# Tile 0 of a PEER layer: every fourth value row weighed by TensorE, with two PSUM banks fewer for the other matmuls

## The chip, the cores and the metric

The kernel runs on one core of one Trainium2 chip. The metric is the device time of one execution in microseconds (us). TensorE is called PE below (PEld is its weight load), VectorE is DVE, ScalarE is ACT, GpSimd is POOL and SyncE is SP, as in the profile.

## The reference

One transformer layer over 512 tokens of width 1024, all float32:

```python
xn   = rmsnorm(h, norm1_g); proj = xn @ w_in
h    = h + concat(forgetting_attention(8 heads), differential_attention(4 heads, 2 maps each)) @ w_out
hn   = rmsnorm(h, norm2_g)
q    = hn @ w_q                              # 8 heads, two halves of 128
eidx = two-stage top-16 of q . sub_keys      # 16 experts per token and head, of 16384
hid  = gelu(sum_d u_tab[eidx] * hn) * softmax(top scores)
h    = h + sum_k hid[k] * v_tab[eidx[k]]     # the value rows
out  = rmsnorm(h, final_g)
```

The last part (PEER) gathers, for each token, 8 x 16 rows of u and of v. With 128 tokens (one per partition) as a tile, "one row" below is a gathered 128 x 1024 block: its own expert row for each of the 128 tokens.

## The kernel before

There are four token tiles. Tile 0 makes attention, projections and queries by itself; tiles 1 to 3 make them together as a second group. PEER of tile 0 runs beside the second group's attention, output projection and queries ("hosted"), since its gathers keep DMA busy; PEER of tiles 1 to 3 follows with nothing beside it ("the tail").

The hosted stretch is 32 slots of four rows each (8 heads x 4 groups). A slot has nine gaps. In DVE's order, slot k holds the dots of its own four u rows in gaps 0, 2, 4, 6 (`dot`, L1220), the coefficients of the slot before at gap 1 (`coefs`, L1234) and the adds of the slot before's four v rows in gaps 1, 3, 5, 7 (`add_row`, L1244: h += coef * row). ACT makes the gelu (L928) of the slot's four dots at gap 6. The second group's work is cut into pieces, and a planner with fixed cost shares lays the pieces into the gaps; PE, ACT and DVE each run their part of every piece in this one order, in program order on each engine. By this plan slots 0 to 5 hold tile 0's last queries and the first input projections of tiles 1 to 3; slots 6 to 16 projections and the forgetting attention; slots 17 to 23 the differential attention and most of the output projection; slots 24 to 31 the last output piece, the second norm and the queries. Slots 25 to 31 hold about two `query` pieces (L609, 16 matmul records each) and one `keys` piece (L694, three tiles of four records each) per slot. DVE has no part in `query` and `keys`: ACT copies them out (L877, L888). Of these, query 8 of head 4 stands at gap 2 of slot 28, the keys piece of head 3 at gap 5 and query 9 at gap 7.

PSUM has eight banks: `mm` is a ring of three (mm0, mm1, acc0) that all 160 projection-like results go through in order, `sc_b` a ring of three (sc0, sc1, acc1) for the 64 score maps, `tr` and `o` one each. PE may fill result n only when result n-3 has been copied out. In the profile the third bank of either ring shows as `acc`. A query's or projection's weights are slabs of 1 MB that SP loads (L490) into two places of `w_ring`; a slab is loaded once PE has done with the slab two before it.

POOL issues the hosted gathers in one order: for each row i, u of row i+4 (L531; waits until dot i is done), then v of row i (L538; waits until the add of row i-4 is done). u and v have rings of four rows each. POOL then issues the tail's gathers (L552), which bring u and v of a row together (1 MB) into a ring of 12 places; places 0 to 3 need nothing but their indices, places 4 to 7 (u_ring, v_ring) wait until all hosted dots and adds are done.

In the tail DVE makes the dots (L1228), ACT turns the four coefficients of a group into diagonal matrices (`diag`, L935), and PE adds `diag @ row` into acc0 and acc1, both halves, over all 128 rows of a tile (L760, four matmul records per row). So that the first tile end can use the same code as the others, DVE clears acc0 and acc1 (L1345) after the hosted stretch, and `fin_tile` (L1263) adds acc to h.

## Time and profile before

| | |
|---|---|
| median of 3 runs | 1662.96 us (1656.92 to 1666.79) |
| the profiled execution | 1672.45 us, span 1670.7 us |
| mean granted TensorE clock | 0.895 |
| busy over the span | PE 77%, PEld 40%, DVE 70%, ACT 26%, POOL 47% |
| HBM | 355 GB/s over the span |

The profiled execution is 9.5 us (0.6%) above the median, and 1.8 us of it lies outside of the span. Busy shares are averages over stages of different kind, so the stages have to be read one by one.

### The profile page before, as it was taken

The page shows a single profiled execution, that of the slowest core. Times are in us where ns is not written, and L with a number is a line of the kernel's source. Part 1 is how long each engine was busy: PE and PEld are TensorE (multiplying, and loading weights), DVE is VectorE, ACT ScalarE, POOL GpSimd, SP SyncE. Part 2 cuts the span into 40 slices and gives each one's busy share as a digit, 9 for nine tenths or more (in the row PEclk, how much of TensorE's full clock was granted, in tenths as well). Part 3 has the DMA queues.
Part 4 walks back from the last instruction along what each step waited for, and adds up shares of the span by engine and source line. Part 5 has one row for each costly group of instructions (what it writes and reads, how often), then busy time and mean ns, then how long its engine had stood idle before and what let it go on. Part 6 is the DMA issues. An engine that isn't in the chain of part 4 may idle for free.

```text
span 1670.7 us, 12756 instructions
## 1 busy us (share of the span) xinstructions
PE 1290.0 (77%) x3547; PEld 662.5 (40%) x3547; DVE 1168.5 (70%) x2794; ACT 427.8 (26%) x1045; POOL 787.5 (47%) x650
## 2 busy tenths in 40 slices
PE   6885788899567788577877877876787777777786
PEld 5754556557333455233323333332333333233332
DVE  2125758898899977676666667666676686666664
ACT  2322313333342321222222222222222222222221
POOL 0004545667455675454554444455444454455441
PEclk9987898798677899799999988999999989999999
DMA  9628888899677898899999999999999999999994
GB/s 309 195 78 295 299 310 302 278 330 345 233 262 250 297 390 322 324 422 421 422 421 421 421 422 422 421 422 422 421 422 421 421 397 421 422 422 421 420 423 168
DMA packets 141244, 594.38 MB, mean 356 GB/s; under 512 B 12400, under 2 KB 53368, under 8 KB 92024
## 3 DMA queue, kind: packets, MB, share of 16 engines
q0 software_dynamic: 92160, 536.91, 80.3%
q1 hardware_dynamic: 49016, 56.67, 10.3%
q8 instruction: 30, 0.49, 0.1%
q14 instruction: 38, 0.31, 0.0%
HBM read 591.44 MB, written 2.10 MB: 355 GB/s over the span
## 4 chain that ended last, share of the span: by engine, by line
DMA 28%; DVE 17%; PE 17%; ACT 2%; issue 2%; POOL 0%; DVEq 0%; POOLq 0%
PE acc L760 11%; DMA act_mem<-in_peer_uv_dram,eidx 11%; DMA v_ring<-in_peer_uv_dram,eidx 9%; DMA map_mem<-in_peer_uv_dram,eidx 8%; PE mm L609 3%; PE acc L609 2%; DVE act_mem L1228 2%; DVE v_ring L1228 2%; DVE map_mem L1228 2%; DVE v_all L1228 1%; DVE w_ring L1228 1%; DVE u_ring L1228 1%; DVE onehot L1195 1%; DVE onehot L1188 1%; DVE picked L1199 1%
## 5 line engine op out<-in xcount | busy, mean ns | idle before, releaser
L531 POOL DMA_INDIRECT u_ring<-in_peer_u_dram,eidx x128 | 162.0, 1266 | 259.0 <-DVE gneg L1205 130.1
L928 ACT ACTIVATE gel<-hid 128x4 f32<-128x4 f32 x128 | 26.2, 205 | 766.9 <-DVE hid L1228 723.1
L760 PE MATMUL acc<-v_all,diag 128*128 128x512 f32 x256 | 142.1, 707 | 84.8 <-ACT diag L935 84.8
L538 POOL DMA_INDIRECT v_ring<-in_peer_v_dram,eidx x128 | 154.6, 1207 | 93.0 <-DVE h L1244 64.1
L760 PE MATMUL acc<-u_ring,diag 128*128 128x512 f32 x256 | 138.4, 692 | 75.1 <-ACT diag L935 75.1
L760 PE MATMUL acc<-w_ring,diag 128*128 128x512 f32 x256 | 137.3, 687 | 74.5 <-ACT diag L935 74.5
L1244 DVE SCALAR_TENSOR_TENSOR h<-v_ring,coef,h 128x1024 f32<-128x1024 f32 x128 | 164.3, 1283 | 4.0 <-DMA v_ring<-in_peer_v_dram,eidx 0.6
L1220 DVE CUSTOM_DVE_ANT_0 u_ring<-u_ring,hn 128x1024 f32<-128x1024 f32 x128 | 156.0, 1218 | 8.8 <-DMA u_ring<-in_peer_u_dram,eidx 8.5
L552 POOL DMA_INDIRECT u_ring<-in_peer_uv_dram,eidx x64 | 77.7, 1215 | 146.9 <-PE acc L760 129.0
L552 POOL DMA_INDIRECT w_ring<-in_peer_uv_dram,eidx x64 | 80.9, 1264 | 131.5 <-PE acc L760 127.8
L552 POOL DMA_INDIRECT v_all<-in_peer_uv_dram,eidx x64 | 78.2, 1222 | 128.9 <-PE acc L760 125.8
L609 PE MATMUL mm<-act_mem,w_ring 128*128 128x384 f32 x336 | 122.0, 521 | 13.2 <-DMA w_ring<-in_w_in_dram 4.8
L935 ACT ACTIVATE diag<-ident,coef 128x128 f32<-128x128 f32 x384 | 123.5, 390 | 29.8 <-DVE coef L1234 22.0
L760 PEld LDWEIGHTS acc<-v_all,diag 128*128 128x128 f32 x256 | 55.2, 226 | 170.0 <-issue 155.1
L760 PEld LDWEIGHTS acc<-u_ring,diag 128*128 128x128 f32 x256 | 53.9, 221 | 159.3 <-issue 154.8
L1228 DVE CUSTOM_DVE_ANT_0 v_ring<-v_ring,hn 128x1024 f32<-128x1024 f32 x64 | 77.8, 1224 | 55.1 <-DMA v_ring<-in_peer_uv_dram,eidx 54.9
L760 PEld LDWEIGHTS acc<-w_ring,diag 128*128 128x128 f32 x256 | 53.4, 219 | 157.7 <-issue 153.3
L760 PE MATMUL acc<-v_ring,diag 128*128 128x512 f32 x256 | 115.1, 592 | 0.0
L760 PE MATMUL acc<-map_mem,diag 128*128 128x512 f32 x256 | 115.1, 592 | 0.0
L760 PE MATMUL acc<-act_mem,diag 128*128 128x512 f32 x256 | 115.1, 592 | 0.0
L1228 DVE CUSTOM_DVE_ANT_0 map_mem<-map_mem,hn 128x1024 f32<-128x1024 f32 x64 | 77.7, 1223 | 53.0 <-DMA map_mem<-in_peer_uv_dram,eidx 52.9
L1228 DVE CUSTOM_DVE_ANT_0 act_mem<-act_mem,hn 128x1024 f32<-128x1024 f32 x64 | 77.7, 1224 | 51.3 <-DMA act_mem<-in_peer_uv_dram,eidx 51.3
(212 smaller groups left out, 2243.6 us busy)
## 6 DMA issues: line engine op xcount, KB each, us to landing
w_ring<-in_w_in_dram SPq DMA_DIRECT2D x18, 1024.0 KB
w_ring<-in_peer_w_q_dram SPq DMA_DIRECT2D x16, 1024.0 KB
v_ring<-in_w_in_dram SPq DMA_DIRECT2D x6, 1024.0 KB, 12.2
w_ring<-in_w_out_dram SPq DMA_DIRECT2D x6, 1024.0 KB
h<-in_x_dram SPq DMA_DIRECT2D x4, 512.0 KB, 6.5
v_ring<-in_w_out_dram SPq DMA_DIRECT2D x2, 1024.0 KB, 5.0
u_ring<-in_peer_u_dram,eidx POOLq DMA_INDIRECT x128
v_ring<-in_peer_v_dram,eidx POOLq DMA_INDIRECT x128
```

The lines of the kernel that those rows point to most:

```text
L531: nc.gpsimd.indirect_dma_start(out=u_ring[:, c % U_RING, :], out_offset=None, in_=peer_u[0], in_offset=bass.IndirectOffsetOnAxis(ap=eidx[n ...
L538: nc.gpsimd.indirect_dma_start(out=v_ring[:, c % V_RING, :], out_offset=None, in_=peer_v[0], in_offset=bass.IndirectOffsetOnAxis(ap=eidx[n ...
L552: nc.gpsimd.indirect_dma_start(out=row_mem[place], out_offset=None, in_=peer_uv, in_offset=bass.IndirectOffsetOnAxis(ap=eidx[n % 3][:, c:c ...
L609: last = nc.tensor.matmul(bk[:, 0:n], w[:, c, q * P:(q + 1) * P], actT[:, c, 0:n], start=(c == 0), stop=(c == KC - 1))
L760: last = nc.tensor.matmul(acc[half][:, :], diag[:, c % COLS, :], v_row(n, c)[:, half * BANK:(half + 1) * BANK], start=(n % PH == 0 and c = ...
L928: nc.scalar.activation(gel[:, par, g0:g0 + COLS], hid[:, par, g0:g0 + COLS], ACT.Gelu).then_inc(gelu_done, 1)
L935: nc.scalar.activation(diag[:, c, :], ident[:, :], ACT.Copy, scale=coef[:, par, g0 + c:g0 + c + 1]).then_inc(diag_done, 1)
L1188: nc.vector.tensor_tensor(out=onehot[:, :, :], in0=top_hlf[:, :, :].rearrange("p a b -> p (a b)").unsqueeze(2).broadcast_to([P, 2 * TOPK, ...
L1195: nc.vector.tensor_tensor(out=oh, in0=oh, in1=tk_if[:, q, :].unsqueeze(1).broadcast_to([P, TOPK, TOPK]), op=ALU.mult).then_inc(topk_step, 1)
L1220: nc.vector.tensor_tensor_reduce(out=u_ring[:, c % U_RING, :], in0=u_ring[:, c % U_RING, :], in1=hn[:, :], scale=1.0, scalar=0.0, op0=ALU. ...
L1228: nc.vector.tensor_tensor_reduce(out=u_row(n, c), in0=u_row(n, c), in1=hn[:, :], scale=1.0, scalar=0.0, op0=ALU.mult, op1=ALU.add, accum_o ...
L1244: nc.vector.scalar_tensor_tensor(out=ht, in0=v_ring[:, c % V_RING, :], scalar=coef[:, par, c:c + 1], in1=ht, op0=ALU.mult, op1=ALU.add).th ...
```

## The change

In tile 0 every fourth value row (c = 3, 7, 11, 15 of each head, 32 of 128) is no longer added by DVE. ACT makes its diagonal (`mixed_diag`, in gap 4 of the next slot, the last one after all pieces), and PE adds it into acc0 and acc1 (`mixed_row`, in gap 7 of the next slot, the last one after all pieces), with a semaphore of its own, `v_mixed`. acc0 and acc1 are in use from the first of these rows on, so the rings `mm` and `sc_b` shrink to two banks each for the whole kernel. The gather of such a row waits for `v_mixed` of the one before, the other gathers count DVE's adds without them (`used`). The clearing of acc0 and acc1, with the waits before it, goes. Tile 0's end waits for both semaphores. Slabs, pieces, gaps and shares stay. The diff, without a few counting lines:

```diff
@@ -381,8 +381,8 @@
         acc = [bank("acc0"), bank("acc1")]
-        mm = [bank("mm0"), bank("mm1"), acc[0]]
-        sc_b = [bank("sc0"), bank("sc1"), acc[1]]
+        mm = [bank("mm0"), bank("mm1")]
+        sc_b = [bank("sc0"), bank("sc1")]
         tr_b = bank("tr")
         o_b = bank("o")
@@ -451,6 +452,15 @@
             return w
         HOSTED = HOSTS * PH * TOPK
+
+        MIXED = HOSTED // COLS
+
+        def used(n, c):
+
+            i = TOPK * n + c
+            if i < HOSTED:
+                return (COLS - 1) * (i // COLS) + min(i % COLS + 1, COLS - 1)
+            return i + 1 - MIXED
         def row_place(n, c):
@@ -534,7 +544,10 @@
             def gather_v(n, c):
                 if n or c >= V_RING:
-                    pool.wait_ge(v_used, TOPK * n + c + 1 - V_RING)
+                    if c % COLS == COLS - 1:
+                        pool.wait_ge(v_mixed, GRP * n + c // COLS)
+                    else:
+                        pool.wait_ge(v_used, used(n, c - V_RING))
                 nc.gpsimd.indirect_dma_start(
                     out=v_ring[:, c % V_RING, :], out_offset=None, in_=peer_v[0],
                     in_offset=bass.IndirectOffsetOnAxis(ap=eidx[n % 3][:, c:c + 1], axis=0)).then_inc(v_in[c % V_RING], 16)
@@ -543,10 +556,11 @@
                 place, lap = row_place(n, c)
                 if lap > 1:
-                    pool.wait_ge(v_used, TOPK * n + c + 1 - ROW_RING)
+                    pool.wait_ge(v_used, used(n, c - ROW_RING))
                 elif place == EARLY_ROWS:
                     pool.wait_ge(dot_done, HOSTED)
-                    pool.wait_ge(v_used, HOSTED)
+                    pool.wait_ge(v_used, used(PH * HOSTS - 1, TOPK - 1))
+                    pool.wait_ge(v_mixed, MIXED)
                 elif place == FREED_ROWS:
                     pool.wait_ge(mm_full, len(MM))
                 nc.gpsimd.indirect_dma_start(
@@ -755,11 +769,22 @@
                         pe.wait_ge(acc_drained, 2 * (n // PH))
                     place, lap = row_place(n, c)
                     pe.wait_ge(row_in[place], 16 * lap)
-                    pe.wait_ge(diag_done, TOPK * n + c + 1 - HOSTED)
+                    pe.wait_ge(diag_done, MIXED + TOPK * n + c + 1 - HOSTED)
                     for half in range(2):
                         last = nc.tensor.matmul(acc[half][:, :], diag[:, c % COLS, :], v_row(n, c)[:, half * BANK:(half + 1) * BANK],
                                                 start=(n % PH == 0 and c == 0), stop=(n % PH == PH - 1 and c == TOPK - 1))
                     last.then_inc(v_used, 1)
+
+            def mixed_row(k):
+
+                c = COLS * (k % GRP) + COLS - 1
+                pe.wait_ge(v_in[c % V_RING], 16 * (k + 1))
+                pe.wait_ge(diag_done, k + 1)
+                for half in range(2):
+                    last = nc.tensor.matmul(acc[half][:, :], diag[:, k % COLS, :],
+                                            v_ring[:, c % V_RING, half * BANK:(half + 1) * BANK],
+                                            start=(k == 0), stop=(k == MIXED - 1))
+                last.then_inc(v_mixed, 1)
             pe.wait_ge(pool_const, 6)
             pe.wait_ge(g1_in, 16)
@@ -770,8 +795,11 @@
                 for n in range(PH * tile, PH * tile + PH):
                     for grp in range(GRP):
                         for gap in range(GAPS):
+                            if gap == 2 * COLS - 1 and (n or grp):
+                                mixed_row(GRP * n + grp - 1)
                             for p_ in pieces_in(n, grp, gap):
                                 piece(*p_)
+            mixed_row(MIXED - 1)
             for n in range(PH * HOSTS, HEADS):
                 for grp in range(GRP):
                     peer_group(n, grp * COLS)
@@ -931,9 +959,20 @@
                 gelu(n, par, g0)
                 act.wait_ge(coef_done, GRP * n + g0 // COLS + 1)
                 for c in range(COLS):
-                    act.wait_ge(v_used, TOPK * n + g0 + c + 1 - COLS)
+                    if TOPK * n + g0 < HOSTED + COLS:
+                        act.wait_ge(v_mixed, MIXED)
+                    else:
+                        act.wait_ge(v_used, used(n, g0 + c - COLS))
                     nc.scalar.activation(diag[:, c, :], ident[:, :], ACT.Copy,
                                          scale=coef[:, par, g0 + c:g0 + c + 1]).then_inc(diag_done, 1)
+
+            def mixed_diag(k):
+                act.wait_ge(coef_done, k + 1)
+                if k >= COLS:
+                    act.wait_ge(v_mixed, k + 1 - COLS)
+                c = COLS * (k % GRP) + COLS - 1
+                nc.scalar.activation(diag[:, k % COLS, :], ident[:, :], ACT.Copy,
+                                     scale=coef[:, k // GRP % 2, c:c + 1]).then_inc(diag_done, 1)
             def fin_rt(t):
                 act.wait_ge(fin_step, FIN * t + 1)
@@ -948,6 +987,8 @@
                 for n in range(PH * tile, PH * tile + PH):
                     for grp in range(GRP):
                         for gap in range(GAPS):
+                            if gap == 2 * COLS - 4 and (n or grp):
+                                mixed_diag(GRP * n + grp - 1)
                             if gap == 2 * COLS - 2:
                                 gelu(n, n % 2, grp * COLS)
                             for p_ in pieces_in(n, grp, gap):
@@ -956,6 +997,7 @@
                             fin_rt(tile - 1)
                         if grp == 2:
                             gate_exp(n + 1)
+            mixed_diag(MIXED - 1)
             for n in range(PH * HOSTS, HEADS):
                 for grp in range(GRP):
                     peer_group(n, n % 2, grp * COLS)
@@ -1330,19 +1375,15 @@
                             elif gap < GAPS - 1 and k > 0:
                                 if c == 0:
                                     coefs(*behind)
-                                add_row(behind[0], behind[1], behind[2] + c)
+                                if c < COLS - 1:
+                                    add_row(behind[0], behind[1], behind[2] + c)
                             if k == PH * GRP * tile and gap == GAPS - 1 and tile:
                                 fin_tile(tile - 1)
                             for p_ in pieces_in(n, grp, gap):
                                 piece(*p_)
                 coefs(n, par, grp * COLS)
-                for c in range(COLS):
+                for c in range(COLS - 1):
                     add_row(n, par, grp * COLS + c)
-
-                dve.wait_ge(*emptied(MM[-1]))
-                dve.wait_ge(*emptied(next(u for u in reversed(MM) if u[0] not in ON_SCALAR)))
-                for half in range(2):
-                    link(nc.vector.memset(acc[half][:, :], 0.0))
             for n in range(PH * HOSTS, HEADS):
                 t, par = n // PH, n % 2
                 if n % PH == 0:
```

## Rows read from the trace of the kernel before

**Rows 1.** Busy sums by stretch: start:end length, PE PEld DVE ACT POOL, clock, DMA share, GB/s.

```profile
0.00:137.30 137.30, 106.91 (x451) 80.22 (x452) 38.47 (x131) 37.97 (x110) 5.50 (x14) 0.91 0.62 197
137.30:255.60 118.30, 93.11 (x328) 62.20 (x327) 77.51 (x164) 29.97 (x61) 56.86 (x49) 0.86 0.83 297
255.60:420.90 165.30, 148.66 (x598) 100.56 (x596) 146.16 (x300) 59.84 (x126) 107.53 (x89) 0.88 0.91 323
420.90:555.00 134.10, 89.56 (x269) 46.24 (x270) 123.73 (x271) 47.58 (x97) 69.96 (x55) 0.75 0.73 251
555.00:686.30 131.30, 104.90 (x372) 64.86 (x370) 99.73 (x188) 30.84 (x69) 82.53 (x65) 0.92 0.92 336
686.30:1670.70 984.40, 746.87 (x1536) 308.43 (x1536) 682.88 (x1745) 221.60 (x583) 465.11 (x380) 0.92 0.98 407
```

**Rows 2.** Chain that ended last: start us, us, what.

```profile
721.96 13.78 DMA v_ring<-in_peer_uv_dram,eidx
...
1635.11 18.40 DMA act_mem<-in_peer_uv_dram,eidx
...
1655.78 7.12 PE acc L760 x16
```

**Rows 3.** Timeline at the hosted stretch's end: start us, us, engine line op tiles [idle before <-releaser].

```profile
681.67 0.16 DVE L1234 TENSOR_TENSOR coef<-gel,gate 128x4 f32<-128x4 f32 x1 [7.49 <-ACT gel L928]
...
681.92 5.53 DVE L1244 SCALAR_TENSOR_TENSOR h<-v_ring,coef,h 128x1024 f32<-128x1024 f32 x4
...
687.56 0.48 DVE L1345 MEMSET acc<- 128x512 f32 x1
688.23 0.94 POOL L552 DMA_INDIRECT u_ring<-in_peer_uv_dram,eidx  x1 [11.79 <-DVE h L1244]
```

**Rows 4.** DVE's timeline in slot 12: adds between dots.

```profile
349.98 1.28 DVE L1244 SCALAR_TENSOR_TENSOR h<-v_ring,coef,h 128x1024 f32<-128x1024 f32 x1
351.19 1.22 DVE L1220 CUSTOM_DVE_ANT_0 u_ring<-u_ring,hn 128x1024 f32<-128x1024 f32 x1
```

**Rows 5.** ACT's diagonals, line L935: min/median/max ns.

```profile
L935 ACT ACTIVATE diag<-ident,coef x384: 384/386/402, 695.2 to 1656.1; 128x128 f32<-128x128 f32 x192
```

**Rows 6.** PE's timeline in the query stage.

```profile
607.25 5.40 PE L609 MATMUL mm<-act_mem,w_ring 128*128 128x384 f32 x16 [1.83 <-issue]
...
622.50 7.09 PE L609 MATMUL acc<-act_mem,w_ring 128*128 128x384 f32 x16 [1.99 <-issue]
...
649.14 5.40 PE L609 MATMUL mm<-act_mem,w_ring 128*128 128x384 f32 x16 [1.39 <-ACT qyT L877]
...
664.38 7.09 PE L609 MATMUL acc<-act_mem,w_ring 128*128 128x384 f32 x16 [3.34 <-issue]
```

**Rows 7.** Timeline of DVE and PE in slots 28 and 31.

```profile
622.09 1.27 DVE L1244 SCALAR_TENSOR_TENSOR h<-v_ring,coef,h 128x1024 f32<-128x1024 f32 x1
...
630.32 0.61 PE L694 MATMUL acc<-subkT,qyT 128*128 128x128 f32 x4
...
668.98 1.28 DVE L1244 SCALAR_TENSOR_TENSOR h<-v_ring,coef,h 128x1024 f32<-128x1024 f32 x1
...
674.12 5.40 PE L609 MATMUL mm<-act_mem,w_ring 128*128 128x384 f32 x16 [1.32 <-ACT store L888]
```

**Rows 8.** PE's waits for score banks, 137 to 690 us: us in total, times, longest.

```profile
PE sc L719 <- DVE negmax L1102: 15.7, 4, 7.8
```

**Rows 9.** Timeline of SP, PE and ACT around the keys of head 4.

```profile
636.12 12.03 SPq L490 DMA_DIRECT2D w_ring<-in_peer_w_q_dram  x2
...
641.09 0.61 PE L694 MATMUL acc<-subkT,qyT 128*128 128x128 f32 x4
641.29 0.49 ACT L877 ACTIVATE qyT<-mm 128x384 f32<-128x384 f32 x1 [4.67 <-PE mm L609]
...
641.53 1.06 PE L694 MATMUL mm<-subkT,qyT 128*128 128x128 f32 x8
641.73 0.38 ACT L888 ACTIVATE store<-acc 128x256 f32<-128x256 f32 x1
```

10 lines of the change are left out of this document (7 added, 3 removed).

## The prediction

> **What bounds the kernel now.** I read the busy sums by stretch first, because the whole-span shares mix stages. The span falls into the part before the hosted rows (0 to 137.3 us), four hosted stretches (slots 0 to 5, 6 to 16, 17 to 23, 24 to 31 with the stretch's end), and the tail from 686.3 us on [rows 1]. In the tail DMA is busy 98% at 407 GB/s, and the chain that ended last alternates between a gather and the group that waited for it, from 721.96 to the last 7.12 us of matmuls [rows 1, 2]. The change touches nothing there. The tail starts with the gather of place 4, issued at 688.23 when the hosted adds had ended [rows 3], so its end moves one for one with the end of the hosted adds, and the question is only where that lies.
>
> In the hosted stretches no single engine is the bound; the reader is to see how the order of the two busiest changes [rows 1]:
> - slots 0 to 5, 118.3 us: PE 93.1, DVE 77.5, DMA 83%: PE first.
> - slots 6 to 16, 165.3 us: PE 148.7, DVE 146.2, DMA 91%: all three at about nine tenths.
> - slots 17 to 23, 134.1 us: DVE 123.7 (92%), PE 89.6 (67%): DVE alone.
> - slots 24 to 31, 131.3 us: PE 104.9, DVE 99.7, DMA 92%: PE's query pieces, and its waits for a slab between them [rows 6].
>
> **What one moved row costs and saves.** DVE: an add takes 1.28 us, but the next dot starts 1.21 us after it [rows 4], so 1.2 us is saved per row, 38 us over 32. PE: four rows are the 16 matmul records of 7.12 us in the chain [rows 2], so 1.78 us per row back to back. A query piece took 5.40 us after one wait and 7.09 after another [rows 6], the difference that the lower of the clock's two levels (1.2 and 2.4 GHz) makes in part of a piece; 32 rows are 57 us, more where the mean clock is below 1. ACT: one diagonal is 0.39 us [rows 5], 12 us in all, with ACT busy a quarter to a third [rows 1]: hidden as time, not as order (below). So 1.2 us on one engine is traded for 1.8 on another, and the place decides: it pays where DVE alone bounds, and costs where PE does. By the plan 5, 11, 7 and 8 of these rows fall into the four stretches, and the last one behind all pieces.
>
> **Stretch by stretch, against the profiled execution's 1672.45 us.**
>
> Before 137.3 us no row moves, but both bank rings are shorter. The nearest rows are those of the keys, where a fill began 0.25 us before the result two before it was copied out [rows 9]; by the order of the pieces some ten fills and the eight score maps of tile 0's differential attention follow that closely here, 18 x 0.25 = 4.5 us. PE is busy 106.9 of 137.3 us [rows 1], and the rest is waits for slabs and for the norms, which hides part. I take +1.5; bounds 0 and +5.
>
> Slots 0 to 5: 5 x 1.78 = +9 on PE, less what fits into its waits (25 us of idle, partly for slabs), and 5 x 1.2 = -6 where DVE leads. PE leads, with waits that hold about half of its part. +3; bounds -6 and +9.
>
> Slots 6 to 16: PE would need 148.7 + 11 x 1.78 = 168.3 us in 165.3, DVE 146.2 - 13.2 = 133. Part of PE's time is the low clock (0.88 on average), and with fewer waits some of this comes back: at the full clock the same work is 148.7 x 0.88 = 131 us. DVE was as full as PE, so its share pays too. +4; bounds -13 (all of the adds) and +20 (all of the rows).
>
> Slots 17 to 23: 7 x 1.2 = -8.4 for DVE. PE has 44 us of idle for 7 x 1.78 = 12 us and, at a clock of 0.75 [rows 1], up to 17. The score ring loses a bank just where every step fills two maps; PE already waits 15.7 us for DVE to empty sc0 and sc1, up to 7.8 at a time [rows 8], in which time DVE is busy with other work, so most of a longer wait costs nothing, but the maps come later after it. -6; bounds -8.4 and +5.
>
> Slots 24 to 31: 8 x 1.78 = +14.2 on PE, which is the path here. The keys piece of three tiles ran through three banks; with two, the second tile waits until ACT has copied the query (641.29 + 0.49 = 641.78 against its start at 641.53), the third until the first is copied [rows 9], and ACT has a diagonal to make between: some 0.5 us for each of 8 heads, +4. Against this stand PE's waits for slabs, 1.83, 1.99, 1.39 and 3.34 us [rows 6]: a slab is asked for when PE ends the one two before it (at 648 us) and used at 664.38 [rows 6, 9], so some 2.2 us more work per slab (1.78 and the copies' half) fills each of the waits by up to 2.2 us, -7.4 in all, and one of the two slow restarts (7.09 - 5.40) goes, -1.7. Slot 24 is DVE work, -1.2. That is +8. Then the release: PE runs behind DVE here. In slot 28 the fourth add started at 622.09, but PE ends the keys piece, behind which the moved row stands, at 630.9 [rows 7]. In slot 31 the add ended at 670.3 and PE gets to the place, behind query 15, at 679.5 [rows 7]: the lag grows from 7.5 to 9.2 us. POOL issues in one order, so behind the gather that waits for this row the next u and v gathers queue too, on a DMA that is 92% busy. I take +2 for it. +10; bounds +1 and +24.
>
> The end: three adds instead of four in 5.53 us, -1.4 [rows 3]. The clearing (from 687.56) stands behind the adds, beside the gathers, and frees nothing that the tail waits for. The last moved row ends on PE at about 684 to 686.5 us, no later than DVE's third add. -1.3; bounds -2.5 and 0.
>
> The wait for the row's diagonal is new on PE, and everything that PE has queued stands behind it. DVE makes the coefficients at gap 1 and ACT the diagonal at gap 4, PE comes to it at gap 7; only where PE is more than six gaps ahead of DVE, in a stretch led by DVE, does it wait, and there DVE is late anyway. I cost it at nothing; without that cover it would be up to 2 us in such a slot.
>
> Sum: 1.5 + 3 + 4 - 6 + 10 - 1.3 = +11.2 us. That is 1683.7 for the profiled execution and, put on the median, 1662.96 + 11 = 1674 us.
>
> **Two rules of the Trainium skill.** In the slots 6 to 16 PE is busy 90% by its matmuls, and its weight loads 100.6 of 165.3 us, 61% [rows 1]. The Trainium skill, Perfetto Trace Analysis, section "Identifying the Most-Contended Engine", holds that the busy share of matmuls is no measure of how near PE is to its limit, and wants the weight loads' share beside it. By that rule PE has room for the rows there, and the stretch would end at its bound of -13 instead of +4; this is rival 1.
> The clock in the slots 17 to 23 is 0.75 against 0.88 before [rows 1], where PE waits for emptied banks. The Trainium skill, TensorE: Matmul & The Clock Gate, section "A second HAM failure mode: psum-queue depth-cycling", says that going round a few PSUM banks leaves TensorE idle briefly and so often that its clock falls again and again, which costs throughput. This speaks against the change; it is the slow rival below.
>
> **The rivals.**
> 1. DVE's time pays wherever it is at nine tenths, and PE's rows vanish in its waits and in a better clock. For it: PE's idle time in the four hosted stretches is 549 - 436.2 = 113 us [rows 1] against 57 to be placed, and 148.7 us of PE time hold only 131 us of full-clock work. Against it: in the query stage the idle time is not there. It gives 1.5 - 3 - 13 - 8 + 8 - 1.3 = -16: 1647 us.
> 2. Slower by much: two banks take PE's lead. If in the slots 6 to 16 the clock fell from 0.88 to the 0.75 of the next stretch, PE's 131 us would take 175 instead of 149, +26 before a row is added, of which I count half, with +12 for the rows; with the late releases (+14 in the query stage) and nothing gained in the slots 17 to 23: 2 + 5 + 25 + 0 + 14 - 1 = +45, 1708 us; with a quarter of the clock's effect 1701. It decides from where PE's wait for an emptied bank lasts longer than PE was ahead of the engine that empties it; the longest such wait now is 7.8 us [rows 8].
> 3. Nothing measurable: DMA is the real limit of the slots 6 to 16 and 24 to 31 (91 and 92%), and both engines' shifts fall into its slack: +1 + 1 + 0 - 5 + 5 - 1 = +1, 1664 us.
>
> **How the numbers follow.** The forecast has 0.42 (its own range 1665 to 1684), rival 1 has 0.20, rival 2 has 0.17, rival 3 has 0.21. The likeliest gives 1674 us. The range is 1645 to 1701: it takes in rivals 1 and 3 and rival 2 up to its milder form, and leaves out some 0.17. About 0.5%, 8.3 us, is what a measurement of this kernel can tell from no change. Faster by more: rival 1 and a little of the rest, 0.22. Within it: rival 3 and the forecast's lower third, 0.32. Slower by more: 0.46.
>
> **What would show it.** In the profile after, DVE has 96 adds at L1244 and PE 128 more matmul records; the same six stretches should read: slots 17 to 23 shorter, slots 24 to 31 longer, slots 6 to 16 within a few us, with PE busy above 95% there. POOL's waits at the v gather should name PE where they named DVE. The forecast is wrong if the slots 6 to 16 shrink by ten us or more (then PE's busy time was no measure), if PE's clock falls below 0.85 there (then the banks count), or if the query stage does not grow (then the slab waits had room for all).

## The result and the profile after

The changed kernel takes 1692.12 us (median of 4 runs, 1690.5 to 1693.0) against 1664.8 for the one before: a ratio of 1.0158, 95% interval 1.0124 to 1.0191, some 26 us slower. The prediction was 1674 with a range of 1645 to 1701 and slower as the likeliest sign. So the sign held and the size fell short by more than half: the result lies outside the forecast's own range (1665 to 1684) and inside the stated one only by the room that was left for the milder form of rival 2. The profiled execution took 1691.76 us with a span of 1690.0 us, 19.3 above the span before; the profiled execution of before was itself above its median, so the tables of spans show some 7 us less than the medians do. Every experiment below was timed beside fresh executions of the kernel before, whose median was 1665.6 to 1670.5 us by the occasion; so the kernels are compared by their ratios to it, and a difference of two raw medians can be off by some 4 us.

The busy sums of the changed kernel in the same six stretches, cut where a slot's first dot starts on DVE and where the tail's normalized input starts (start:end length, PE PEld DVE ACT POOL, clock, DMA share, GB/s):

```profile
0.00:136.00 136.00, 106.80 (x450) 79.24 (x451) 38.57 (x131) 38.18 (x110) 5.44 (x14) 0.92 0.62 199
136.00:257.00 121.00, 100.06 (x336) 64.81 (x335) 71.55 (x159) 31.52 (x65) 53.53 (x49) 0.87 0.82 289
257.00:428.90 171.90, 164.41 (x653) 105.10 (x651) 132.76 (x288) 63.44 (x137) 104.22 (x89) 0.96 0.89 318
428.90:565.30 136.40, 94.67 (x290) 50.03 (x291) 115.94 (x265) 49.09 (x103) 65.68 (x55) 0.79 0.70 238
565.30:700.70 135.40, 119.82 (x414) 72.30 (x413) 90.76 (x180) 34.64 (x79) 75.40 (x65) 0.95 0.85 298
700.70:1690.00 989.30, 754.02 (x1540) 310.83 (x1538) 681.62 (x1743) 222.03 (x583) 457.33 (x382) 0.91 0.99 409
```

The last cut lies at the start of the tail's input here. For before, the same cut is at 688.7 us, 2.4 later than in [rows 1]:

```profile
555.00:688.70 133.70, 104.90 (x372) 64.86 (x370) 101.85 (x190) 30.84 (x69) 83.01 (x66) 0.91 0.90 330
688.70:1670.70 982.00, 746.87 (x1536) 308.43 (x1536) 680.76 (x1743) 221.60 (x583) 464.63 (x380) 0.92 0.98 408
```

Against [rows 1] and these two, the stretches changed by -1.3, +2.7, +6.6, +2.3, +1.7 and +7.3 us. DVE lost its adds everywhere (146.2 to 132.8 in slots 6 to 16), and no hosted stretch became shorter for it. PE took the rows (148.7 to 164.4, 96% of the stretch).

What became of the saved time stands in DVE's waits. In slots 6 to 16 of before, then of the changed kernel (us in total, times, longest):

```profile
DVE map_mem L1102 <- PE sc L723: 8.5, 3, 4.1
DVE map_mem L1102 <- PE acc L723: 5.8, 4, 2.6
```

```profile
DVE map_mem L1144 <- PE sc L737: 30.1, 10, 7.9
DVE rinv L1161 <- PE o L762: 5.4, 1, 5.4
```

DVE was busy 13.4 us less there and waited 21 us more for score maps and for attention's output. Slot 7 shows two such waits, where before it had one of 4.09 us; first PE's, then DVE's timeline of the changed kernel (start us, us, engine, line, tiles, [idle before <-releaser]):

```profile
266.37 1.88 PE L784 MATMUL acc<-v_ring,diag 128*128 128x512 f32 x4
268.09 3.62 PE L615 MATMUL mm<-w_ring,act_mem 128*128 128x256 f32 x16
...
280.89 7.01 PE L623 MATMUL mm<-act_mem,w_ring 128*128 128x384 f32 x16
287.73 1.88 PE L784 MATMUL acc<-v_ring,diag 128*128 128x512 f32 x4
289.54 0.70 PE L733 MATMUL sc<-store 64*128 64x256 f32 x2
```

```profile
273.34 0.42 DVE L1144 CUSTOM_DVE_ANT_0 map_mem<-sc,act_mem 128x256 f32<-128x256 f32 x1 [4.03 <-PE sc L737]
...
290.81 0.42 DVE L1144 CUSTOM_DVE_ANT_0 map_mem<-sc,act_mem 128x256 f32<-128x256 f32 x1 [7.94 <-PE sc L737]
```

The moved row at 287.73 stands between a projection piece and the scores that DVE's next step needs. Before, the scores followed the projection at once. A row takes under 2 us, so it makes only about half of the second wait's growth (4.09 to 7.94); the rest is that PE was already behind when it came to the projection, at 280.89 instead of 276.53 us, and the row of slot 6 (266.37), with which the slot starts, is a part of that. The slot grew from 16.9 to 23.1 us. It is the one that grew most: slots 8 and 9 behind it were 4.5 us shorter together, and over slots 6 to 16 6.6 us are left. In slots 17 to 23 it is the output projection that comes late (before, where a result can also lie in the third bank, `acc`, then after):

```profile
DVE h L1077 <- PE mm L669: 3.7, 3, 3.1
DVE h L1077 <- PE acc L669: 1.2, 1, 1.2
```

```profile
DVE h L1119 <- PE mm L683: 14.4, 6, 3.7
```

[Rows 8] shows PE's waits for two of the three score banks. The third stands in a row of its own; here it is, and behind it the changed kernel's, which has two banks only:

```profile
PE acc L719 <- DVE negmax L1102: 7.5, 1, 7.5
```

```profile
PE sc L733 <- DVE negmax L1144: 27.2, 9, 8.4
```

So with a bank less PE waits 27.2 us instead of 23.2 for DVE to empty a score bank, and no wait is much longer than before.

At the end of the hosted stretch, answering [rows 3], POOL and DVE of the changed kernel:

```profile
695.86 0.94 POOL L551 DMA_INDIRECT v_ring<-in_peer_v_dram,eidx  x1 [8.45 <-PE acc L784]
697.10 1.63 POOL L566 DMA_INDIRECT v_all<-in_peer_uv_dram,eidx  x1 [0.30 <-issue]
...
704.06 0.94 POOL L566 DMA_INDIRECT u_ring<-in_peer_uv_dram,eidx  x1 [1.25 <-PE acc L784]
...
736.62 1.85 POOL L566 DMA_INDIRECT u_ring<-in_peer_uv_dram,eidx  x1 [10.02 <-PE acc L774]
```

```profile
696.64 4.12 DVE L1287 SCALAR_TENSOR_TENSOR h<-v_ring,coef,h 128x1024 f32<-128x1024 f32 x3
700.68 1.28 DVE L1294 SCALAR_TENSOR_TENSOR hn<-h,rstd,g2b 128x1024 f32<-128x1024 f32 x1
704.60 1.23 DVE L1271 CUSTOM_DVE_ANT_0 v_all<-v_all,hn 128x1024 f32<-128x1024 f32 x1 [2.64 <-DMA v_all<-in_peer_uv_dram,eidx]
```

The gather of the last moved row (695.86) waited 8.45 us for PE's row before it, and the tail's first four gathers stand behind it in POOL's one order. Before, the tail's first gather went out at 671.8, 17 us ahead of the tail's input; here it is 3.6 us ahead, and the first dots wait for their rows. The last moved row itself waited 2.79 us for its gather and ended on PE at 703.3, 2.5 us behind DVE's third add; the gather of place 4 (704.06) waits for it. The tail's 17th gather (the one at 736.62) stood at 717.31 before. From it to the end both kernels take 953.4 us. So all 19.3 us lie ahead of it: 12.0 up to the tail's input, and 7.3 between that and the 17th gather (28.6 us before, 35.9 after).

One limit of these tables: kernels with the same order of work up to a place can be compared up to there. Three of those below have one order up to slot 17, and single executions of them take 164.7, 164.8 and 167.7 us in slots 6 to 16. The changed kernel and the one where the tail's gathers go first have one order up to the last value gather, and take 171.9 and 178.3 there. So a difference of one pair under 3 us says nothing by itself, and one of 6 to 7 can be chance too. That slots 6 to 16 grow with the rows on PE rests on many kernels: the eight that have full or thin rows there, or their work, read 171.6 to 186.5, and the six that don't read 161.7 to 167.7.

### The profile page after: what moved, and what is told of

Its sections match the earlier page's. It is cut to its first block, busy times and chain, and to the rows that moved or that the text cites. A ratio compares the mean times of both kernels' runs of the same rounds, so it can differ in the third digit from the quotient of the medians.

```text
span 1690.0 us, 13041 instructions
## 1 busy us (share of the span) xinstructions
PE 1339.8 (79%) x3675; PEld 682.3 (40%) x3675; DVE 1131.2 (67%) x2760; ACT 438.9 (26%) x1077; POOL 761.6 (45%) x650
## 4 chain that ended last, share of the span: by engine, by line
DMA 28%; PE 21%; DVE 15%; ACT 2%; issue 2%; POOL 1%; DVEq 0%; POOLq 0%
PE acc L774 12%; DMA map_mem<-in_peer_uv_dram,eidx 12%; DMA act_mem<-in_peer_uv_dram,eidx 9%; DMA v_ring<-in_peer_uv_dram,eidx 7%; PE mm L623 5%; PE mm L683 2%; DVE act_mem L1271 2%; DVE map_mem L1271 1%; DVE v_ring L1271 1%; PE acc L784 1%; DVE u_ring L1271 1%; DVE w_ring L1271 1%; DVE onehot L1237 1%; DVE onehot L1230 1%; DVE picked L1241 1%
## 5 line engine op out<-in xcount | busy, mean ns | idle before, releaser
L541 POOL DMA_INDIRECT u_ring<-in_peer_u_dram,eidx x128 | 150.0, 1172 | 256.0 <-DVE gneg L1248 128.9
L551 POOL DMA_INDIRECT v_ring<-in_peer_v_dram,eidx x128 | 149.2, 1166 | 138.7 <-PE acc L784 64.9
L774 PE MATMUL acc<-w_ring,diag 128*128 128x512 f32 x256 | 145.0, 719 | 76.5 <-ACT diag L966 71.8
L623 PE MATMUL mm<-act_mem,w_ring 128*128 128x384 f32 x512 | 174.8, 499 | 3.2 <-DVE act_mem L1055 1.6
L566 POOL DMA_INDIRECT w_ring<-in_peer_uv_dram,eidx x64 | 73.7, 1152 | 140.6 <-PE acc L774 138.5
L966 ACT ACTIVATE diag<-ident,coef 128x128 f32<-128x128 f32 x384 | 123.9, 390 | 31.5 <-DVE coef L1277 22.0
L623 PEld LDWEIGHTS mm<-act_mem,w_ring 128*128 128x128 f32 x512 | 98.8, 196 | 74.7 <-issue 12.4
L1287 DVE SCALAR_TENSOR_TENSOR h<-v_ring,coef,h 128x1024 f32<-128x1024 f32 x96 | 123.1, 1283 | 4.5 <-DMA v_ring<-in_peer_v_dram,eidx 0.6
L615 PE MATMUL mm<-w_ring,act_mem 128*128 128x256 f32 x416 | 107.2, 418 | 7.2 <-DVE act_mem L1055 5.1
```

Source lines behind the costliest of these rows:

```text
L541: nc.gpsimd.indirect_dma_start(out=u_ring[:, c % U_RING, :], out_offset=None, in_=peer_u[0], in_offset=bass.IndirectOffsetOnAxis(ap=eidx[n ...
L551: nc.gpsimd.indirect_dma_start(out=v_ring[:, c % V_RING, :], out_offset=None, in_=peer_v[0], in_offset=bass.IndirectOffsetOnAxis(ap=eidx[n ...
L566: nc.gpsimd.indirect_dma_start(out=row_mem[place], out_offset=None, in_=peer_uv, in_offset=bass.IndirectOffsetOnAxis(ap=eidx[n % 3][:, c:c ...
L615: last = nc.tensor.matmul(bk[:, 0:SLAB], actT[:, c, j * P:(j + 1) * P], w[:, c, :], start=(c == 0), stop=(c == KC - 1))
L623: last = nc.tensor.matmul(bk[:, 0:n], w[:, c, q * P:(q + 1) * P], actT[:, c, 0:n], start=(c == 0), stop=(c == KC - 1))
L774: last = nc.tensor.matmul(acc[half][:, :], diag[:, c % COLS, :], v_row(n, c)[:, half * BANK:(half + 1) * BANK], start=(n % PH == 0 and c = ...
```

## The experiments

The theory at the start (Theory A in the first expectations) was that the rows on TensorE carry most of the loss and the rings a few us. Beside it stood the late release of the moved rows' buffer and the start of the tail.

### The rings alone, and the rows alone

```diff
-        mm = [bank("mm0"), bank("mm1"), acc[0]]
-        sc_b = [bank("sc0"), bank("sc1"), acc[1]]
+        mm = [bank("mm0"), bank("mm1")]
+        sc_b = [bank("sc0"), bank("sc1")]
```

> The kernel before with two banks in each ring and no row moved: one half of the change alone. Theory A (most of the 27 us comes from the moved rows: their PE time and the later releases) expects what the prediction gave the banks: 1.5 us before slot 0 and 4 us in the query stage, so +3 to +9 us over before. Theory B (the lost banks take PE's lead) expects at least half of the loss, +13 to +25 us, most of it in slots 6 to 23. If the banks cost nothing, within 2 us of before.

Measured: 1677.16 us, ratio 1.0058 (1.0032 to 1.0085), so some 10 us of the 26 (5 to 14).

The counterpart keeps the three-bank rings of the kernel before and has the rows:

```diff
-        mm = [bank("mm0"), bank("mm1")]
-        sc_b = [bank("sc0"), bank("sc1")]
+        mm = [bank("mm0"), bank("mm1"), acc[0]]
+        sc_b = [bank("sc0"), bank("sc1"), acc[1]]
...
+                pe.wait_ge(*emptied(MM[filled[0] - len(mm)]))
                 for half in range(2):
-                    last = nc.tensor.matmul(acc[half][:, :], diag[:, k % COLS, :],
+                    last = nc.tensor.matmul(mm[filled[0] % len(mm)][:, :], diag[:, k % COLS, :],
```

> The other half alone: the 32 rows go to PE in the same places, with the same waits and the same DVE saving, but both rings keep three banks. The moved rows are written into the mm bank that the next result will overwrite, so their part of tile 0's sum is left out, and acc0 and acc1 are cleared as before. Theory A expects +18 to +24 us over before (the change's 27 less the banks' 3 to 9). Theory B expects at most +13 us, or even a gain.

Measured: 1690.28 us, ratio 1.0149 (1.0095 to 1.0203). The rows bring nearly the whole loss with the longer rings too. With the rings' 10 us this makes 35 where 26 were measured; the intervals leave it open whether the two causes add. One part of this stays open: a row here has to find the next products' bank empty, a wait that the changed kernel doesn't have.

### The rows' time on PE

```diff
+                n = BANK if k == 0 else 8
                 for half in range(2):
-                    last = nc.tensor.matmul(acc[half][:, :], diag[:, k % COLS, :],
-                                            v_ring[:, c % V_RING, half * BANK:(half + 1) * BANK],
+                    last = nc.tensor.matmul(acc[half][:, 0:n], diag[:, k % COLS, :],
+                                            v_ring[:, c % V_RING, half * BANK:half * BANK + n],
```

> The change with PE's time for the moved rows taken away: 31 of the 32 rows are multiplied over 8 columns per half instead of 512 (the first over all), every wait, place, bank and the DVE saving stay. The rest of those rows is left out of tile 0's sum. If PE's 57 us of extra work is what costs, -15 to -27 us against the change. If the order costs (releases behind PE, the tail's first gathers behind the last moved row, DVE waiting for score maps), -3 to -10 us.

Measured: 1687.85 us, ratio 1.0128 (1.0082 to 1.0173), only 5 us under the changed kernel by the ratios (4 by the medians), less than their intervals can tell. The groups of PE in slots 6 to 16, first of the changed kernel, then of this one (xcount | busy us, mean ns of one | idle before):

```profile
L623 PE MATMUL mm<-act_mem,w_ring 128*128 128x384 f32 x128 | 46.1, 516 | 0.0
...
L784 PE MATMUL acc<-v_ring,diag 128*128 128x512 f32 x44 | 21.2, 604 | 2.1 <-DMA v_ring<-in_peer_v_dram,eidx 1.2 <-ACT diag L974 1.0
```

```profile
L623 PE MATMUL mm<-act_mem,w_ring 128*128 128x384 f32 x128 | 52.9, 576 | 0.0
...
L785 PE MATMUL acc<-v_ring,diag 128*128 128x8 f32 x44 | 6.1, 248 | 2.2 <-DMA v_ring<-in_peer_v_dram,eidx 1.2 <-ACT diag L975 1.0
```

The rows lost 15.1 us of PE time, and PE was busy 163.3 us instead of 164.4: the other pieces took 14 us more, with a granted clock of 0.88 instead of 0.96. So in these slots the run could not separate PE's time from its order; what the rows gave up in columns the clock took from the others. In slots 24 to 31 it was otherwise: PE was busy 112.1 us instead of 119.8, at a clock of 0.91 instead of 0.95, and the stretch took 129.4 us instead of 135.4.

### PE's work alone, and DVE's saving alone

These three take the change apart in another way. The first is the rings alone plus PE's work at the rows' places, which nothing waits for but the clearing of acc0 and acc1 at the end:

```diff
+            def more_pe(k):
+                for half in range(2):
+                    last = nc.tensor.matmul(acc[half][:, :], ident[:, :], g2b[:, half * BANK:(half + 1) * BANK],
+                                     start=(k == 0), stop=(k == GRP * PH * HOSTS - 1))
...
+                            if gap == 2 * COLS - 1 and (n or grp):
+                                more_pe(GRP * n + grp - 1)
```

> The kernel before with two-bank rings (as in the run of the rings alone), where TensorE also does 32 pairs of full-width products of the size and at the places of the moved rows, on resident data into the two free banks; nothing waits for them and nothing reads them, and VectorE still adds all four rows of a group. So TensorE's work is that of the change, without its releases and without what VectorE saves. The rings alone gave 1677 us. Theory P: TensorE's 57 us of added work lengthen slots 6 to 16 by 5 to 8 us and the rest by 2 to 6: 1685 to 1691. Theory R: TensorE's work alone costs little: 1677 to 1681, slots 6 to 16 at 164 to 167 us.

Measured: 1695.33 us, ratio 1.0155 (1.0117 to 1.0192). That is the whole loss of the change, with no late release and nothing saved. Against the rings alone, PE's added work costs 16 us by the ratios, give or take 8. Its slots 6 to 16:

```profile
263.00:435.80 172.80, 166.38 (x648) 105.90 (x646) 146.00 (x300) 60.07 (x126) 106.17 (x89) 0.94 0.89 315
```

DVE does all its adds here (146.0) and the stretch is as long as in the changed kernel, where it does three quarters of them (132.8 in 171.9). Theory P held: by the ratio the time is 1691 us on the scale of 1664.8, the upper end of what it gave. That PE alone sets the stretch is not shown by this, since the changed kernel also has late releases that may have taken what DVE's saving gave; the next run bears on it.

The second is the changed kernel with VectorE's saving undone, by adding each group's third row twice:

```diff
+                if c % COLS == COLS - 2:
+                    link(nc.vector.scalar_tensor_tensor(out=ht, in0=v_ring[:, c % V_RING, :], scalar=coef[:, par, c:c + 1], in1=ht,
+                                                        op0=ALU.mult, op1=ALU.add))
```

> The changed kernel, where VectorE adds the third row of each group twice, so that its work is again that of four adds (the third row counts double in tile 0's output; TensorE still weighs the fourth). It asks what VectorE's saving of 32 adds at 1.2 us, 38 us in sum, is worth. If it had been worth its length on the path, the time would rise by 38 us to 1730. The forecast put it on the path only in slots 17 to 23, worth about 6 us net and 9 us by itself. If the saved time only turns into waits for TensorE's results and for loads, the time stays within 4 us of 1692. I expect 3 to 8 us: 1695 to 1700, most of it in slots 17 to 23.

Measured: 1703.99 us, ratio 1.0229 (1.0184 to 1.0275). The saving is worth about 12 us in the changed kernel (3 to 21 by the two intervals), more than the 3 to 8 that I had expected, and not 38. In the profile it shows in slots 6 to 16 (178.9 us against 171.9) and 17 to 23 (139.1 against 136.4). The 7 us are no more than two executions of one order differed by above, but they are spread otherwise: eight of the eleven slots are each 1.0 to 1.6 us longer, about an add, where the chance difference lay in two slots. So DVE's adds still lie on the path in most slots there, and PE's time isn't the only bound.

The third is the change without its costs: the kernel before, with the fourth add cut to eight columns.

```diff
-                ht = h[:, n // PH, :]
-                nc.vector.scalar_tensor_tensor(out=ht, in0=v_ring[:, c % V_RING, :], scalar=coef[:, par, c:c + 1], in1=ht,
+                w = 8 if c % COLS == COLS - 1 else D
+                ht = h[:, n // PH, 0:w]
+                nc.vector.scalar_tensor_tensor(out=ht, in0=v_ring[:, c % V_RING, 0:w], scalar=coef[:, par, c:c + 1], in1=ht,
```

> The kernel before, with three-bank rings and no row on TensorE, where VectorE's add of a group's fourth row takes 8 of its 1024 columns in tile 0 (so that row is left out of the sum but for 8 columns); its gather, its buffer and the order are as before. It is the change without its costs, so it gives the most that moving the adds could be worth. The run with TensorE's added work alone and the changed kernel differ by 9.9 us in the length of the part with tile 0's work (710.6 against 700.7), and the changed kernel with VectorE's saving undone differs by the same 10 us (710.8). If the saving is worth the same here: 1655 (1651 to 1659), 2 to 4 us of it in slots 17 to 23. The forecast's terms put 9 us into slots 17 to 23 alone. If instead TensorE's rows hide a larger worth, and VectorE bounds more slots once nothing is added on TensorE, up to half of the 38 us comes out: 1640 to 1650.

Measured: 1659.69 us, ratio 0.9964 (0.9936 to 0.9992): the offload, free of charge, is worth 6 us, between 1 and 11. (An add of 8 columns isn't nothing: DVE was busy 33 us less in the hosted slots, against 38 less in the changed kernel.) Its slots 6 to 16 and 17 to 23:

```profile
248.60:410.30 161.70, 148.43 (x603) 100.68 (x601) 134.95 (x300) 59.89 (x126) 104.61 (x89) 0.89 0.93 330
410.30:541.30 131.00, 88.61 (x269) 46.04 (x270) 116.54 (x271) 46.97 (x97) 67.48 (x55) 0.75 0.75 257
```

Even in slots 17 to 23, where DVE was busy 92% [rows 1], 7.2 us less of DVE made the stretch 3.1 us shorter, which is at the edge of what a pair of executions can tell. DVE's waits for the output projection rose there from 4.9 to 9.1 us (both kinds of bank), with nothing added on PE. The largest difference was in slots 0 to 5, 113.2 us against 118.3.

### The late release

On PE and on ACT:

```diff
-                            if gap == 2 * COLS - 1 and (n or grp):
+                            if gap == 2 * COLS - 4 and (n or grp):
-                            if gap == 2 * COLS - 4 and (n or grp):
+                            if gap == 2 * COLS - 6 and (n or grp):
```

> The changed kernel with the diagonal of the moved row built at gap 2 and the row weighed at gap 4 of the slot behind, instead of gaps 4 and 7; the arithmetic is the same. So far: the two-bank rings alone cost about 10 us, the rows with three-bank rings 22 to 25 us, and rows of eight columns, which take hardly any of TensorE's time, gave back only 4 us. Theory R (release): what costs beside the banks is that the gather of a group's fourth row, and everything behind it on GpSimd's queue, waits for TensorE's row of the group before, which stands late in the slot. Then the release three gaps earlier cuts GpSimd's waits for TensorE (65 us in sum in the changed kernel) to about half, and the time falls by 5 to 9 us, to 1683 to 1687. Theory P (TensorE's time and order): what costs is that TensorE's own chain of pieces is longer in the slots where it works without a break. Then the earlier place changes nothing (within 3 us of 1692), or costs 2 to 5 us where the row now stands in front of scores that VectorE waits for.

Measured: 1712.74 us, ratio 1.0254 (1.0213 to 1.0294): 16 us slower than the change by the ratios (20 by the medians), where a gain of 5 to 9 or a loss of 2 to 5 was expected. GpSimd's waits for TensorE did fall, from 56 to 9 us. But now PE waits for the row itself, and everything behind it in PE's order waits too (waits between 136 and 690 us):

```profile
PE acc L784 <- DMA v_ring<-in_peer_v_dram,eidx: 23.4, 5, 7.4
```

```profile
DVE map_mem L1144 <- PE sc L737: 39.3, 13, 6.7
```

Slots 6 to 16 took 186.5 us. Of the two places, gap 7 is the better by far.

The next takes the release away instead, with a second buffer (`fin`) for every other moved row:

```diff
+        def mixed_mem(k):
+            return fin if k % 2 else v_ring[:, COLS - 1, :]
...
+                    if k > 1:
+                        pool.wait_ge(v_mixed, k - 1)
```

> The changed kernel, but the moved rows alternate between two buffers (the fourth place of the value ring, and the buffer of the final output, which nothing uses in tile 0), so that the gather of a moved row waits for the row two groups before, which is long done. Nothing else is changed. Theory R: GpSimd's waits for TensorE at the value gathers fall from 65 us to under 10 us, and what the late release cost comes back: 1692 falls to 1678 to 1684, with slots 6 to 16 at 165 to 168 us (171.9 in the changed kernel) and the stretch after tile 0's part 3 to 6 us shorter. Theory P: GpSimd's waits fall too, but slots 6 to 16 stay at 170 to 172 us, and only the start of the tail gains, 0 to 4 us: 1688 to 1692.

Measured: 1693.62 us, ratio 1.0152 (1.0113 to 1.0191), no gain. GpSimd's waits at that gather went:

```profile
POOL fin L554 <- PE acc L793: 0.6, 2, 0.3
```

and from the tail's input to its 17th gather it is 28.7 us again, 7.2 less than in the changed kernel. But slots 6 to 16 took 172.8 us, as theory P says, and slots 0 to 5 took 124.7 against 121.0, with 8.0 us of waits for weight slabs on PE against 1.0. These waits differ much from kernel to kernel in that stretch, 4.8 us in the one before and 7.1 in the one with the thin add. Whether the gathers, now free to go out sooner, delayed those slabs, or the execution fell so by chance, no run tells.

Two runs ask only for the end. In the first, the tail's first four gathers go ahead of the last value gather:

```diff
+                    if TOPK * n + c == HOSTED - 1:
+                        numbers_of(n + 1)
+                        for early in range(EARLY_ROWS):
+                            gather_row(n + 1, early)
```

> The change with one order altered: POOL issues the first four gathers of the tail before the last value gather of tile 0, which waits for the 31st moved row. In the profile after they stand behind it (697 to 702 us; before the change at 672 to 675 us, ahead of the end of the hosted stretch), DMA is idle meanwhile and the tail reads 989.3 us against 982.0. Theory A expects that these four rows (10 us of DMA) come back in large part: -5 to -9 us. If the tail's length differs for another reason (PE's clock, another restart of the rings), 0 to -2 us.

Measured: 1697.11 us, ratio 1.0181 (1.0138 to 1.0223): no gain that could be seen. The tail's gathers came earlier (the first at 694.2 with its input at 707.2), but the last moved row, now behind 4 MB of them, held PE:

```profile
710.74 3.78 PE L789 MATMUL acc<-v_ring,diag 128*128 128x512 f32 x4 [7.01 <-DMA v_ring<-in_peer_v_dram,eidx]
```

It ended at 714.5, and place 4's gather, which waits for it, went out at 715.3. The wait moved from one gather to the other. From the tail's input to its 17th gather it is 31.4 us, 4.5 less than in the changed kernel, but the rest took 960.7, the longest of all. Of the 9.3 us that this profiled execution lies above the changed kernel's, 6.4 are in slots 6 to 16, where the edit does nothing; so the run neither shows a gain nor a loss.

### Where the rings and the rows cost

```diff
-        mm = [bank("mm0"), bank("mm1"), acc[0]]
+        mm = [bank("mm0"), bank("mm1")]
```

> The kernel before with two banks for TensorE's products alone; the scores keep three. Two banks for both cost 9.7 us (interval 5 to 14). If it is the products' ring that TensorE's lead in the long projections hangs on: 6 to 10 us slower than before, 1671 to 1675, most of it in slots 17 to 24. If it is the scores' ring (TensorE's scores waited 28 us for VectorE in that run, against 16 us before): 0 to 3 us, 1665 to 1668. I expect the scores' ring to carry the greater part, so 1667.

Measured: 1678.19 us, ratio 1.0081 (1.0057 to 1.0105), as much as both rings together within the intervals. So it is the products' ring, and I had expected the scores'. The waits of PE in slots 17 to 23 with both rings short point to a place; before, the same wait was 0.8 us:

```profile
PE mm L589 <- DVE h L1077: 5.1, 2, 3.8
```

The transposes of the second norm need a bank that DVE empties with its add of the output projection (h, L1077), and DVE is late in that stretch. It took 137.4 us (137.3 with the products' ring alone) against 134.1. That is 3 of the 10 to 13 us; where the rest is lost the spans don't show. PE's waits for the score banks, all three counted, grew from 23.2 to 25.8 us there with both rings short, and cost nothing that the run of the products' ring alone lacks. The ring of scores was not shortened alone.

Then the rows only where PE has room by its busy share:

```diff
+        FROM = 17
+        MIXED = HOSTED // COLS - FROM
...
+                            if gap == 2 * COLS - 1 and GRP * n + grp > FROM:
```

> The changed kernel, where only the 15 groups of slots 17 to 31 have their fourth row weighed by TensorE; in slots 0 to 16, where TensorE works almost without a break, VectorE adds all four. If the costs add up by stretch: slots 0 to 16 as with the two-bank rings alone (421.6 us to slot 17), slots 17 to 31 and the end as in the changed kernel (271.8 us, then 989): 1683, so 9 us faster than the change and still 18 us slower than before. The forecast's term of -6 us for slots 17 to 23 would show as a length of 128 to 131 us for these against 137 with the rings alone. If the late release at the end of tile 0's part (7 us by the stretch after it) is all that is left, and the rows in slots 24 to 31 cost nothing: 1680.

Measured: 1685.42 us, ratio 1.0126 (1.0068 to 1.0184), against 1683 expected. The stretches from slot 17 on:

```profile
420.50:557.10 136.60, 93.93 (x286) 49.82 (x287) 117.00 (x265) 48.84 (x102) 67.11 (x55) 0.78 0.72 246
557.10:692.00 134.90, 119.40 (x413) 72.08 (x412) 90.54 (x180) 34.68 (x79) 73.73 (x65) 0.95 0.85 298
692.00:1681.50 989.50, 753.04 (x1540) 309.94 (x1539) 681.33 (x1743) 221.73 (x583) 454.63 (x382) 0.92 0.99 409
```

The spans agree with costs that add up by stretch. With the rows only here, slots 17 to 23 are 0.8 us shorter than with the rings alone, slots 24 to 31 are 2.2 longer and the stretch behind them 8.4 longer (981.1 there): the last 15 rows cost 11 us by the ratios (8 by the medians), and the tail's start is where most of it shows. The first 17 rows cost the other 5 (7 by the medians). Either figure has an interval of some 11 us either way, so the times alone don't show this split.

Last, the same with a buffer of its own for the last moved row alone:

```diff
+                if TOPK * n + c == HOSTED - 1:
+                    nc.gpsimd.indirect_dma_start(
+                        out=fin[:, :], out_offset=None, in_=peer_v[0],
+                        in_offset=bass.IndirectOffsetOnAxis(ap=eidx[n % 3][:, c:c + 1], axis=0)).then_inc(last_in, 16)
+                    return
...
-                    pool.wait_ge(v_mixed, MIXED)
+                    pool.wait_ge(v_mixed, MIXED - 1)
```

> The run with rows from slot 17 on, where the last moved row alone is gathered into a buffer of its own (that of the final output, unused in tile 0), so that its gather and the tail's first gathers behind it on GpSimd's queue don't wait 8.5 us for TensorE's row before it; all else is the same. In the runs so far the time from the tail's first normalized input to the tail's 17th gather is 28.6 to 29.5 us where the last value gather doesn't wait for TensorE, and 35.4 to 35.9 us in the changed kernel and in the run with rows from slot 17 on. If that wait is what the stretch behind tile 0's part lost: that stretch falls from 989.5 to 982 to 984, and the time from 1685.4 to 1677 to 1680, about that of the two-bank rings alone. If the wait is hidden and something else lengthens the stretch (TensorE's last rows, the clock): 1683 to 1687.

Measured: 1683.52 us, ratio 1.0118 (1.0079 to 1.0157). The mechanism is there: its last value gather went out with no wait, the time from the tail's input to the 17th gather fell from 35.4 to 28.9 us, and from slot 17's start to that gather it is 301.5 us against 306.9. The gain in time, 1.3 us by the ratios (1.9 by the medians), is below what the runs can tell, so of the 7 us at the tail's start a trace puts 5.4 down to the late release, and the times none; the hosted part ended later in the same profile (697.4 against 692.0, of which 4.3 us had come before slot 17). What speaks for the trace is that the time from the tail's input to the 17th gather is 34.8 to 35.9 us in four kernels where the last value gather waits 5.8 to 8.5 us for PE, and 28.6 to 29.6 in the eight where it waits under 2 us for PE or not at all. The kernel with the rows and three-bank rings has the wait and reads 31.0; there the tail's input itself stands behind the last row. No version here beats the kernel before but the one that leaves the work out.

## Why the prediction was right in sign and short in size

By its own steps, in spans (forecast, then what the profile or a run showed):

- **Per row.** DVE 1.2 us and ACT 0.39 held, with 96 adds and 128 more records of PE. PE's 1.78 held where its clock was full (a row stands in the timeline with 1.88 us); over all 32 rows its records were busy 67.5 us, 2.1 a row, as "more where the mean clock is below 1" had said. That 1.2 is traded for 1.8 was the right frame, and slower the right sign.
- **Before slot 0**, +1.5: -1.3, nothing measurable. The ten close fills between tile 0's pieces cost nothing.
- **Slots 0 to 5**, +3: +2.7. The number is luck. The term was priced for the rows, and with the rings alone, no row moved, the stretch reads 120.8 us, +2.5, where the forecast had put nothing for the rings; and the waits for weight slabs, 4.8 us before and 1.0 after, are in the difference too.
- **Slots 6 to 16**, +4: +6.6. It took the stretch to be shared by both engines. PE's work alone makes it 8 us longer than the rings alone do (172.8 against 164.7), and undoing DVE's saving makes the changed kernel's 7 us longer (178.9 against 171.9). The part with the clock was right: 0.88 rose to 0.96, and 15.7 us of PE work lengthened the stretch by less than half of that.
- **Slots 17 to 23**, -6: +2.3. This is the step that failed, by 8 us. "DVE alone" was read off a busy share of 92%, and the adds were counted at their full length. What the waits show instead is that PE waits there for DVE (25.2 us for score banks) and ACT (16.1 us for maps), and DVE for PE's output projection (14.4 us), so each holds up the other in turn; with the adds gone for free it gave 3.1 of 7.2 us, and what was left went for the products' bank (+3.2), of which I had priced only the scores', at almost nothing. The remaining 2 us are less than a pair of executions can tell.
- **Slots 24 to 31**, +10, and the end, -1.3: +1.7 together. PE's busy time rose by 14.9 us, as forecast (14.2). But its idle time fell from 28.8 to 15.6 us, more than the 9.1 that I had given the slabs and the restart: in the profile after, one wait of 0.37 us is left in front of a query piece and every piece takes 5.3 to 5.4 us ([rows 6] had four waits and two of 7.09). The +4 for the banks at the keys pieces did not come: with the rings alone the stretch is 132.7 against 133.7. Nor did the +2 for the release show: with two buffers, which take it away, the stretch reads 135.2. The prediction had named a query stage that doesn't grow as a sign that it is wrong, since then the slab waits had room for all; with +1.7 that is nearly what came.
- **The tail's start.** "Its end moves one for one with the end of the hosted adds" failed, and 7.3 us came from there that stand in no term. The link held for place 4's gather while the four before it lay long ready. I had seen that gathers queue behind the moved row's release, priced it at +2 inside slots 24 to 31, and did not follow the queue one step on, to the tail's first four gathers behind the last value gather. The last moved row was to end no later than DVE's third add, and ended 2.5 us behind it.
- **The wait for the diagonal**, 0: 1.0 us in all.

The sum missed the spans' 19.3 us by 8, which is partly luck. Slots 17 to 23 and the tail's start came out 8 and 7 us above their terms, slots 24 to 31 with the end 7 us below theirs, and the first of these is as large as the whole miss.

Slow rival 2 had one half right, that banks cost (10 us), but not by the clock: with two banks it is 0.89 and 0.75 in the middle stretches, against 0.88 and 0.75 before. The Trainium skill's page TensorE: Matmul & The Clock Gate, section "A second HAM failure mode: psum-queue depth-cycling", names a cost that the trace does not show in these two stretches. In slots 0 to 5 it isn't settled: 0.86 before and with both rings short, but 0.82 with the products' ring alone, which took 123.9 us there and waited 6.5 us for a slab. Over the whole kernel the mean clock of these runs is 0.892 and 0.891, against 0.895 and 0.896 for the kernel before beside them; whether that is a cause or a consequence of the lost time stays open. Rival 1 rested on PE having room at 90% busy by matmuls and 61% by weight loads. The stretch went to 96% and grew. The Trainium skill, Perfetto Trace Analysis, section "Identifying the Most-Contended Engine", says that the matmuls' busy share is not a good measure of how close TensorE is to its roofline, and names the weight loads' share, beside the share of peak FLOPs, in its place. In this stretch the 61% of weight loads misled rival 1: of the 15.7 us of added matmuls 9.1 went into PE's idle time (16.6 us before, 7.5 after) and 6.6 lengthened the stretch. The page is borne out in so far as a busy share of 90% took in more than half of them, at a clock that rose.

The ledger by the ratios of the medians: the rings 0.6% (10 us); PE's work on top 1.0% (16 us); release, diagonals and PE's waits for the rows 0.7% (12 us, the run with the saving undone against the one with PE's work alone; 9 by their medians); DVE's saving -0.7% (-12 us). The sum is 26, the measured loss, but that is no test: each item is the difference of two neighbours in a row of four kernels, so they must add up to it. Their intervals are 4 us either way for the rings and 8 to 10 for the others. That the release, the diagonals and the waits are worth 9 to 12 is not shown by the two runs that took the release away, in whole or at the end, and gained nothing; it stays open what these 12 us are.

## What to carry to other kernels

Before an operation is moved off an engine, take it away without replacing it: the free version here gave 6 us for 33 us of busy time taken away. Six (1 to 11) is then, as far as this run tells, about the most that moving the adds could gain, and PE's added work, as placed here, cost 16. A busy share above nine tenths on an engine that exchanges small results with others in a fixed order is not a bound by itself; ask what that engine will wait for once it is faster. And where a release moves to another engine, follow the issuing queue behind it to its end, into the next stage.

## What the hardware did that I had not expected

- The granted clock rose when PE was given more to do: 0.88 to 0.96 in slots 6 to 16 and 0.91 to 0.95 in the query stage with full rows. With thin rows of 8 columns in the same places it was 0.88 and 0.91, and the projection's records took 576 ns on average instead of 516 in slots 6 to 16, so that there PE time taken away came back as slower work elsewhere.
- One of three banks in the ring of products cost 13 us (9 to 18) in a kernel where PE waits for a bank only a few times. Taking one from the ring of scores as well, whose waits are longer in sum, added no cost that the runs can tell (10 us, 5 to 14, for both).
- In this kernel's last stage DMA is busy 98 to 99%, and from its 17th gather on thirteen of the fourteen kernels, before, after and the variants, took 952.0 to 957.1 us (the other, with the tail's gathers first, 960.7): what was done before shows there mostly as a shift.
